# Twelve more kilobytes per partition: some rows of the first expert pair loaded early, and third slots in halves

## What is computed

```python
def expert_block(args):
    tok, e = args
    hcat = xf[tok] @ w1[e] + b1[e]                 # 1024 -> 2048
    h_glu = jnp.minimum(hcat[:, :D_FF_2], SWIGLU_LIMIT)
    h_lin = jnp.clip(hcat[:, D_FF_2:], -SWIGLU_LIMIT, SWIGLU_LIMIT)
    act = h_glu * jax.nn.sigmoid(SWIGLU_ALPHA * h_glu) * (h_lin + 1)
    return act @ w2[e] + b2[e]                     # 1024 -> 1024
...
y = jax.ops.segment_sum(y_buf.reshape(n_buf, d) * buf_w[:, None], buf_tok, num_segments=n_tok)
```

## Time and profile before

| | |
|---|---|
| median of 3 runs | 2051.35 us (2049.64 to 2051.96) |
| span of the profiled execution | 2047.8 us; the page gives no other time of it, and the median lies 3.55 us above |
| PE busy | 1938.0 us, 95% of the span, x11046 |
| DVE, ACT busy | 915.7 us (45%), 644.4 us (31%) |
| DMA | 589.90 MB in 45164 packets, mean 288 GB/s |
| expert weights, whole slots | 68 + 23 transfers of 4096 KB, median 29.8 us from issue to landing |
| granted clock of PE | 0.991 |

### The profile page before, as it was taken

One profiled execution on the slowest core, in us unless ns is written; L12 is line 12 of the kernel. 1 busy time (PEld: TensorE's weight loads), 2 busy tenths in 40 slices (PEclk: granted clock), 3 DMA queues, 4 the chain that ended last, 5 costly groups with the idle time before them and its releaser, 6 DMA issues.

```text
span 2047.8 us, 26788 instructions
## 1 busy us (share of the span) xinstructions
PE 1938.0 (95%) x11046; PEld 1281.3 (63%) x11046; DVE 915.7 (45%) x1565; ACT 644.4 (31%) x1086; POOL 10.6 (1%) x24
## 2 busy tenths in 40 slices
PE   8999999999998999999999999999999989899888
PEld 8979998979996677877898333333333333333332
DVE  6877677977766337456656211111111111111112
ACT  5565556565556324355644100000000000000001
POOL 0000000010000000000000000000000000000000
PEclk9999999999999999999999999999999999999999
DMA  8345544445546644031448999999999999999997
GB/s 316 118 165 199 185 165 168 153 180 207 185 165 267 244 172 171 32 122 43 157 176 356 372 421 433 433 432 431 430 431 432 433 432 433 430 431 431 432 432 309
DMA packets 45164, 589.90 MB, mean 288 GB/s; under 512 B 5328, under 2 KB 6032, under 8 KB 10960
## 3 DMA queue, kind: packets, MB, share of 16 engines
q1 hardware_dynamic: 43296, 583.09, 69.7%
q0 software_dynamic: 1488, 5.28, 0.9%
q10 hardware_dynamic: 288, 0.24, 0.0%
HBM read 587.54 MB, written 1.05 MB: 287 GB/s over the span
## 4 chain that ended last, share of the span: by engine, by line
PE 73%; DMA 20%; DVE 3%; ACT 3%; issue 1%; SPq 0%; DVEq 0%; ACTq 0%
PE psum L2113 46%; PE psum L2589 19%; DMA slots<-exp_w_dram 11%; DMA work<-exp_w_dram 7%; PE psum L2534 3%; PE psum L2715 3%; DVE split_weights L1635 0%; DMA slots<-ada_w_dram 0%; DVE work L1461 0%; ACT work L959 0%; ACT split_rows L988 0%; ACT split_weights L1145 0%; DVE work L1779 0%; PE psum L2133 0%; PE psum L2260 0%
## 5 line engine op out<-in xcount | busy, mean ns | idle before, releaser
L2589 PE MATMUL psum<-slots,work 128*64 128x512 f32 x2304 | 516.4, 600 | 52.4 <-DMA slots<-exp_w_dram 44.2
L2113 PE MATMUL psum<-split_rows,split_weights 128*128 128x256 f32 (+1 forms) x3792 | 506.3, 295 | 6.4 <-DVE split_rows L1402 3.4
L2113 PEld LDWEIGHTS psum<-split_rows,split_weights 128*128 128x128 f32 x3792 | 483.9, 192 | 31.0 <-issue 11.0
L2589 PEld LDWEIGHTS psum<-slots,work 128*64 128x64 f32 x2304 | 166.8, 138 | 364.8 <-issue 329.6
L1423 DVE TENSOR_TENSOR split_weights<-slots,split_weights 128x1024 fp32r<-128x1024 f32 x180 | 219.5, 1223 | 121.3 <-ACT split_weights L1003 120.4
L1003 ACT ACTIVATE split_weights<-slots 128x1024 fp32r<-128x1024 f32 x180 | 190.4, 1062 | 184.8 <-PE psum L2113 164.8
L2113 PE MATMUL psum<-split_weights,split_rows 128*128 128x512 f32 x1008 | 233.5, 391 | 0.0
L2113 PEld LDWEIGHTS psum<-split_weights,split_rows 128*128 128x128 f32 x1008 | 188.3, 188 | 41.9 <-issue 3.3
L2078 DVE TENSOR_SCALAR work<-psum 128x512 f32<-128x512 f32 x32 | 22.0, 687 | 388.3 <-PE psum L2589 388.3
L2589 PE MATMUL psum<-work 128*64 128x512 f32 x768 | 173.0, 603 | 17.1 <-DMA work<-exp_w_dram 17.1
L1331 ACT ACTIVATE work<-work 128x512 f32<-128x512 f32 x32 | 20.2, 631 | 475.4 <-DVE work L2078 475.4
(11 more groups left out here) (284 smaller groups left out, 1360.4 us busy)
## 6 DMA issues: line engine op xcount, KB each, us to landing
slots<-exp_w_dram SPq DMA_DIRECT2D x68, 4096.0 KB, 29.8
work<-exp_w_dram SPq DMA_DIRECT2D x23, 4096.0 KB, 29.8
slots<-w_in_dram SPq DMA_DIRECT2D x56, 1024.0 KB, 6.0
slots<-ffn_up_dram SPq DMA_DIRECT2D x44, 1024.0 KB, 4.8
slots<-ada_w_dram SPq DMA_DIRECT2D x24, 1024.0 KB, 8.6
slots<-ffn_down_dram SPq DMA_DIRECT2D x20, 1024.0 KB, 4.8
slots<-w_out_dram SPq DMA_DIRECT2D x12, 1024.0 KB, 4.8
slots<-exp_w_dram SPq DMA_DIRECT2D x4, 2048.0 KB, 8.6
```

Source lines behind the costliest of these rows:

```text
L2113: return nc.tensor.matmul(out_, lhsT, rhs, start=first, stop=last)
L2589: return nc.tensor.matmul(b[rows, :], lhs[:, rows], rhs, start=first, stop=last, skip_group_check=True)
```

## The change

A tensor `early_rows` of 3 x 1024 floats per partition is added, and the scratch of the dynamic DMA is set to 4096 bytes per partition (the default is 16384), which makes the room. In the first pair, three of the eight rows of slot n = 5 (row 0 of both experts, row 1 of the first) are loaded into it, issued by SP ahead of the wait of slot n = 4; the other five go to the slot's place when it is free, and PE reads the three rows from `early_rows`. In all pairs but the first, slot n = 2 is loaded in two halves, each one row block for both experts. PE releases the first half of that place when it is done with k = 0 and 1 of w2, q = 0 of the pair before.

```diff
+        early_rows = sb("early_rows", 3 * D)
...
-        third_part_loaded = sem("third_slot_part_loaded")
+        early_rows_loaded, w2_half_free, half_pair_loaded = (
+            sem(n) for n in ("early_rows_loaded", "w2_half_slot_free", "w1_half_slot_loaded"))
+        early = {(0, 0): 0, (1, 0): D, (0, 1): 2 * D}
...
@@ SP, pair @@
                     if part == "first" and n == 2:
...
-                        sp.dma_start(to[:, 0:2 * HALF], src[:, 0:2 * HALF]).then_inc(third_part_loaded, 16)
+                        sp.dma_start(to[:, 0:2 * HALF], src[:, 0:2 * HALF]).then_inc(half_pair_loaded, 16)
...
                     elif part == "first" and n == 4:
+                        last_src = w["exp_w2_2"][j, 1].rearrange("p (x k n) -> p x k n", x=2, k=4)
+                        sp.dma_start(early_rows[:, 0:2 * D].rearrange("p (x n) -> p x n", x=2), last_src[:, :, 0, :]
+                                     ).then_inc(early_rows_loaded, 16)
+                        sp.dma_start(early_rows[:, 2 * D:], last_src[:, 0, 1, :]).then_inc(early_rows_loaded, 16)
                         to, src = (v.rearrange("p (x h n) -> p x h n", x=2, h=2) for v in (to, src))
                         sp.wait_ge(first_half_free, 1)
...
+                    elif part == "first" and n == 5:
+                        sp.wait_ge(expert_slot_free, 6 * it + (n + 1))
+                        to, src = (v.rearrange("p (x k n) -> p x k n", x=2, k=4) for v in (to, src))
+                        sp.dma_start(to[:, 1, 1, :], src[:, 1, 1, :]).then_inc(early_rows_loaded, 16)
+                        sp.dma_start(to[:, :, 2:4, :], src[:, :, 2:4, :]).then_inc(loaded, 16)
+                        continue
+                    elif n == 2:
+                        to, src = (v.rearrange("p (x h n) -> p x h n", x=2, h=2) for v in (to, src))
+                        sp.wait_ge(w2_half_free, it)
+                        sp.dma_start(to[:, :, 0, :], src[:, :, 0, :]).then_inc(half_pair_loaded, 16)
+                        sp.wait_ge(expert_slot_free, 6 * it + (n + 1))
+                        sp.dma_start(to[:, :, 1, :], src[:, :, 1, :]).then_inc(loaded, 16)
+                        continue
@@ PE, pair, w1 @@
-                        if part == "first" and q == 2:
-                            pe.wait_ge(third_part_loaded, 16)
+                        if q == 2:
+                            pe.wait_ge(half_pair_loaded, 16 * it + 16)
@@ PE, pair, w2 @@
+                        if part == "first" and q == 1:
+                            pe.wait_ge(early_rows_loaded, 48)
+                            placed = wt
+                            wt = [lambda k, c0, c1, xx=xx: early_rows[:, early[xx, k] + c0:early[xx, k] + c1]
+                                  if (xx, k) in early else placed[xx](k, c0, c1) for xx in (0, 1)]
...
                                 elif xx and (k, n) == (3, 1):
                                     ins.then_inc(expert_slot_free, 1)
+                                elif xx and (q, k, n) == (0, 1, 1):
+                                    ins.then_inc(w2_half_free, 1)
...
-    nc = bacc.Bacc("TRN2", target_bir_lowering=False, num_devices=1)
+    nc = bacc.Bacc("TRN2", target_bir_lowering=False, num_devices=1, dynamic_dma_scratch_size=4096)
```

## The result

The changed kernel takes 2053.99 us in the median of 21 runs (2051.24 to 2057.96), the kernel before 2051.17 us in 21 runs beside it (2047.26 to 2053.86). The medians differ by 2.8 us. The ratio that is estimated from all the runs is 1.0017, with a 95% interval of 1.0011 to 1.0024: 3.5 us slower (2.3 to 4.9). That is clear of zero and a little under the 0.2% that I had set as the line. Forecast were 2054.5 us, +3.2 us.

What follows compares the result with a forecast made beforehand. Expert-weight transfers were taken to bound the kernel once the queue is never dry. Price +4.1 us less gain 0.9 made +3.2 us on 2051.35, about 2054.5 us; range 2050.2 to 2057.0.

Steps and rivals of the forecast that it cites:

- The picture of two parts: Expert stage: in pairs 0 and 1 the queue sometimes runs dry; later it is never dry and PE waits.
- Part 1: Pair 0: 1.57 MB of n = 5 issued early into a 4.3 us hole, charged nothing; later loads move up to 3.6 us.
- Parts 1 and 2 together: Early rows plus n = 2 in halves: pair 1's n = 4 lands earlier, gain 0.9 us (0 to 1.5).
- the start-up: Pair 1's n = 4 load into an empty queue: 2.7 us before its bytes' 9.7 us.
- Part 3: Price of n = 2 in 8 KB pieces: 14 slots x 0.29 = +4.1 us, ends 2.2 and 6.3.
- My row: Last pair's n = 3, already in 8 KB pieces, landing 10.0 us behind its predecessor against 9.71 for whole slots.
- The scratch: Dynamic DMA scratch cut to a quarter: should hold any burst of the software queue's packets, so costs nothing.
- signs of being wrong: n = 2 taking 9.7 us, the issue at 1193.3 coming earlier, or POOL or DVE waiting longer for bias rows.
- D: Rival, chance 0.03: the smaller scratch stalls POOL past 1149.8 us, delaying pair 0 and later issues; about 2060 us.
- A: Rival, chance 0.15: 8 KB pieces are free in a deep queue, so only the gain stays; 2050.4 us.
- B: Rival, chance 0.05: lead survives pair 1's n = 4 issue, end moves up 3.6 plus 0.7 us; 2047.05 with free pieces.
- C: Rival, chance 0.22: pieces cost the slowest row's +6.3 us, gain 0 to 0.9; 2056.8 to 2057.65 us.

Runs made afterwards that it cites:

- the changed kernel with the row block outermost: Changed kernel with expert weights repacked so that a half slot is one contiguous 16 KB piece per partition; ratio 1.0004 against the kernel before.
- rows only: Kernel before plus the early rows and the smaller scratch, without the split n = 2; ratio 1.0002.
- The halves alone: Kernel before plus n = 2 split in 15 pairs, without early rows and with the old scratch; ratio 1.0018.
- the 8 KB and the 16 KB experiment: Kernel before with every slot of pairs 1 to 14 in two transfers issued together, of 8 KB or 16 KB pieces; ratios 1.0096 and 1.0026.
- the three kernels in which two microseconds or more got past both: Changed kernel with n = 2 and 4 halved: odd pairs, repacked, 0.9998; pair 1 only, PE keeping its loop, 1.0003, and repacked, 0.9998, against the kernel before.

## Why the prediction was right, by its own steps

The direction, the price as the cause and its rough size were right. That 3.2 us came so near to the 3.5 measured is in part luck: both terms of the sum were too large, with opposite signs.

**The picture of two parts was right.** PE still has no wait for a transfer between 1140 and 1300 us, and the lead ends where PE still holds up a load with little in the queue ahead of it: at pair 1's n = 4, and where that one comes earlier, at n = 3. (The stretch from slice 24 on is 16 x 51.2 = 819 us, not 830.)

**Part 1, the early rows.** Charged at nothing and worth 3.6 us of bytes that came forward; the hole was filled to 0.92 and the n = 4 load of pair 0 still landed 7.8 us after its issue. Right.

**Parts 1 and 2 together: 0.9 us taken, 0 to 1.5 as ends.** The lead reached pair 1's n = 3 with 2.4 us and ended there. The n = 4 load itself won nothing (13.4 for 13.3 us), and neither did n = 5 (23.1 us after the hinge for 23.0). The next slots landed 0.5 us earlier against the hinge, but so they did in two kernels without early rows, so no run shows a gain. The term that I mis-sized is the start-up: I took 2.7 us from a 2 MB load, and the 4 MB load needs 13.4 - 9.7 = 3.7 us over its bytes. It needs that whether its predecessor landed 3.2 us after its issue (the kernel before) or at its issue (the changed kernel with the row block outermost, issued at 1192.72 with the queue empty since 1192.69, 13.4 us): the emptier queue gives nothing back. With rows only, the ratio holds both zero and -0.9 us.

**Part 3, the price: 0.29 us a slot taken, 4.1 us in sum.** Measured are 0.22 us from landing to landing, 0.26 us a pair by the chain and 0.25 by the rate with all slots in 8 KB pieces, so 14 x 0.25 = 3.5 us with the rate, 3.1 with the landings; the stretch with all 14 of them is 3.2 to 3.5 us longer. The halves alone cost 3.7 us (1.8 to 5.5). My row was read rightly: by the finer stamps the last pair's n = 3 takes 4.98 + 5.03 = 10.01 us before, and 4.99 + 5.02 in the changed kernel. But it is not like a halved slot in mid-stream, which takes 9.93. So the price was 0.6 to 1.0 us too high and the gain, by the traces, 0.9 too high, and in the sum the two nearly cancel.

**The scratch**, at nothing: right, by the kernel with rows only and by the kernel with halves only. One of my signs of being wrong came all the same, DVE's longer wait for the bias rows (1.34 us for 0.89); it comes with the old scratch too (1.50), and POOL's issues take no longer, so it is no sign of D.

**The rivals.** A (pieces are free, 2050.4) falls with the 8 KB and the 16 KB experiment. With it falls the estimate of 0.09 us a slot that I had worked out from the Trainium skill (DMA: Bandwidth & Descriptors, "Why small descriptors are slow"); the runs show 0.25, and 0.08 to 0.09 for each further piece. B (the lead survives) falls with the rows alone, and its condition turned out stricter than I wrote: two issues would have to come earlier, and in the three kernels in which two microseconds or more got past both, 1.5 to 2 us of it was gone a few slots later, for a cause that stays open. C had the right sign, but 5.4 to 6.3 us where 3.5 were measured. D did not happen.

## What to carry to other kernels

Where transfers set the pace, bytes moved forward are worth at most what gets past the last load that still waits for an engine; find that load, and any just ahead of it, before you count bytes. Even what got past it did not reach the end whole here. Halving a transfer for an earlier start costs every time it runs, also where it is never early: here 0.22 to 0.25 us for 4 MB in four pieces per partition instead of one, 0.08 to 0.09 in two, so halve only where the queue would be dry, and pack the data so that the half is contiguous. And cut the execution at the hinge when you compare traces; otherwise one drop of PE's clock ahead of it, 1.7 us, hides a gain of the same size.

## What the runs showed of the hardware that I had not expected

- The rate of a full queue goes by the pieces: 432, 428 and 421 GB/s with 32, 16 and 8 KB per piece.
- A 4 MB load into an empty queue landed 13.4 us after its issue, 3.7 us more than a slot takes behind another in a full one; with a predecessor that was still running for 3.2 us it was 13.3.
- In a full queue single landings came 0.4 to 1.5 us late, and the slots behind them kept the delay. In the slowest of them the engines' share was 1.01 around it. Why is open.
- PE's granted clock fell to 0.5, 1.2 instead of 2.4 GHz, for about 3.4 us in a stretch in which PE was busy but for a wait of 0.69 us, in seven of thirteen profiled executions, one of each kernel; 16 matmuls took 5.35 us instead of 3.65.
